# One transformer pair on one core: attention, value tiles, HGRN output and output projection put in another order on TensorE

## The reference

```python
# attention: 8 heads of 64, three dilated windows, merged by their softmax weights
for window, dilation in ((128, 1), (512, 4), (2048, 16)):
    o, l = dilated_window_attention(qh, kh, vh, window, dilation)   # softmax over keys t, t-d, ..., t-window
...
y = jnp.sum(softmax(lses)[..., None] * outs, axis=0)
# HGRN: 4 heads of 128; o = causal product of decayed scores with the values i
o = o * lax.rsqrt(jnp.mean(o * o, axis=-1, keepdims=True) + NORM_EPS)      # mean over the 128 of a head
o = o.reshape(B, S, HGRN_WIDTH) * norm_w
yb = o * jax.nn.silu(g)
...
mixed = jnp.concatenate([ya, yb], axis=-1)
h = h + jnp.einsum('bse,ed->bsd', mixed, w_out)
```

## Time and profile before

| | |
|---|---|
| median of three runs | 2258.12 us |
| the profiled execution | 2256.9 us, span 2255.1 us |
| TensorE busy | 2164.3 us, 96% |
| VectorE, ScalarE busy | 1521.4 us, 1073.4 us |
| granted TensorE clock, mean | 0.972 |
| last projection tile to end of output projection | 1657.2 to 1879.2 us of the span |

### The profile page before, as it was taken

How to read it: one execution, slowest core, us unless ns; L and a number is a source line. 1 busy time by engine, 2 the same in 40 slices (tenths; PEclk the granted TensorE clock), 3 DMA queues, 4 the chain that set the end, 5 groups by cost and what they waited for, 6 DMA issues and landing times.

```text
span 2255.1 us, 25922 instructions
## 1 busy us (share of the span) xinstructions
PE 2164.3 (96%) x8736; PEld 1432.9 (64%) x8736; DVE 1521.4 (67%) x1575; ACT 1073.4 (48%) x950; POOL 234.9 (10%) x239
## 2 busy tenths in 40 slices
PE   8999999999999999999999999689997899999998
PEld 3445457777777777777777777445643346888886
DVE  3953369999999999999999999544614633333333
ACT  1010147777777777777777777420002423222222
POOL 0003311112111111121211211100000000000000
PEclk9998989999999999999999999889998899999999
DMA  6123379999999999999999999611221011222220
GB/s 255 56 84 114 121 317 340 377 376 382 376 374 381 373 384 373 382 379 373 384 372 381 382 370 380 254 38 38 94 93 47 1 38 56 94 94 98 108 94 37
DMA packets 77756, 522.63 MB, mean 232 GB/s; under 512 B 10208, under 2 KB 10736, under 8 KB 21264
## 3 DMA queue, kind: packets, MB, share of 16 engines
q1 hardware_dynamic: 65088, 483.95, 55.4%
q0 software_dynamic: 9168, 31.01, 5.4%
q10 hardware_dynamic: 3456, 7.06, 1.0%
HBM read 500.98 MB, written 18.99 MB: 231 GB/s over the span
## 4 chain that ended last, share of the span: by engine, by line
PE 90%; DVE 7%; ACT 1%; DMA 1%; issue 1%; SPq 0%; DVEq 0%; ACTq 0%; POOLq 0%
PE bank L1006 21%; PE bank L1008 21%; PE bank L1007 21%; PE bank L872 13%; PE bank L1118 6%; DVE room L1301 3%; PE bank L1022 1%; PE bank L1133 1%; PE bank L1216 1%; PE bank L978 1%; PE bank L1014 1%; PE bank L881 1%; PE bank L1198 1%; DVE room L1640 1%; DVE room L1662 0%
## 5 line engine op out<-in xcount | busy, mean ns | idle before, releaser
L1448 DVE TENSOR_TENSOR ring_r<-ring,room_r 128x2048 fp32r<-128x2048 f32 x384 | 873.3, 2288 | 90.1 <-ACT room_r L626 87.3
L626 ACT ACTIVATE room_r<-ring 128x2048 fp32r<-128x2048 f32 x384 | 735.7, 1917 | 189.0 <-PE bank L1008 183.3
L1006 PE MATMUL bank<-room_r 128*96 128x512 f32 x1536 | 607.1, 395 | 3.5 <-DVE room_r L1480 1.9
L1008 PE MATMUL bank<-room_r 128*96 128x512 f32 x1536 | 603.1, 393 | 0.0
L1007 PE MATMUL bank<-ring_r,room_r 128*96 128x512 f32 x1536 | 603.0, 393 | 0.0
L1008 PEld LDWEIGHTS bank<-room_r 128*96 128x96 f32 x1536 | 248.8, 162 | 105.7
L1006 PEld LDWEIGHTS bank<-room_r 128*96 128x96 f32 x1536 | 248.9, 162 | 105.4 <-DVE ring_r L1448 4.4
L1007 PEld LDWEIGHTS bank<-ring_r,room_r 128*96 128x96 f32 x1536 | 249.0, 162 | 101.0 <-issue 0.2
L872 PE MATMUL bank<-ring,room 128*128 128x512 f32 x544 | 238.9, 601 | 4.0 <-ACT room L587 3.3
L872 PEld LDWEIGHTS bank<-ring,room 128*128 128x128 f32 x544 | 104.7, 194 | 134.5 <-issue 133.5
L1118 PE MATMUL bank<-room,ring 128*128 128x512 f32 x320 | 140.4, 597 | 0.0
(11 more groups left out here) (243 smaller groups left out, 2053.8 us busy)
## 6 DMA issues: line engine op xcount, KB each, us to landing
ring<-in_wmoe SPq DMA_DIRECT2D x384, 1024.0 KB, 11.6
ring<-in_wf SPq DMA_DIRECT2D x33, 1024.0 KB, 4.8
ring<-in_wp SPq DMA_DIRECT2D x9, 2048.0 KB, 7.8
ring<-in_wd SPq DMA_DIRECT2D x7, 2048.0 KB, 8.9
ring<-in_wd SPq DMA_DIRECT2D x3, 1024.0 KB, 8.1
room<-in_xT SPq DMA_DIRECT2D x2, 1024.0 KB, 8.4
room<-in_xtok ACTq DMA_DIRECT2D x1, 2048.0 KB, 7.7
h_rows<-room POOLq DMA_DIRECT2D x4, 512.0 KB, 3.1
```

What stands on the lines that cost most here:

```text
L626: act.activation(w_hi[s_ % PAIRS], raw_w[ORDER[s_]], ACT.Copy)\
L1006: pe.matmul(out, x_hi, w_hi, start=start, stop=False, skip_group_check=True)
L1008: return pe.matmul(out, x_lo, w_hi, start=False, stop=stop, skip_group_check=True)
L1448: dve.tensor_tensor(w_lo[i], raw_w[i], w_hi[s_ % PAIRS].bitcast(F32), ALU.subtract)\
```

## The change

**TensorE.** After the last projection tile it waits for all rotated tiles (`rot_done`, 8) and issues the scores of units 0 to 3 with 8 of the 64 value matmuls behind each. In each of the first 16 units two more value matmuls come first. HGRN output is made per token tile j, with `AT` as weights and tokens on partitions, ahead of units 17, 20, 23 and 26 (`O_AT`). `head_values` of a head moves from the end of its own units to the start of the next head's. After the last unit the output projection starts with three attention columns of groups 0 to 4; between them stand the last `head_values` and four transposes per token tile of the normed HGRN output (`hgrn_turn`); then the rest of all groups, each in a bank of its own.

**VectorE.** The mask `madd` now holds log(count)/SCALE where a key is allowed, so the product with `ctab` goes; `masked` takes a minimum of the negated scores, so that the separate scaling of the maximum goes; the sum comes from ScalarE's exponential. `masked` runs four units ahead, behind `weighted`; before, it ran two ahead, in front of it. The HGRN norm is one reciprocal of 128 x 16 and two products of 128 x 1024 at the end of the attention, and four products with the transposed output; `hg_norm` moves into the gate's product.

**ScalarE.** The exponentials run four units ahead and accumulate their sum. `probs_out` copies 512, 512 and 256 columns in place of 512, 384, 256 and 128. The value copies lie among the units, and after units 17, 20, 23 and 26 come a copy of 512 columns and four squares of 128 with their sums (`hgrn_evac`). One root of 128 x 16 stands behind the last `probs_out`.

**SP.** The table c2 is 1536 columns wide in place of 2048. The third feed-forward weight waits for the end of the scores and of `hgrn_turn`. The last norm's row is loaded during the feed-forward part, since its buffer holds attention output now.

```diff
+O_AT = [17, 20, 23, 26]
...
                 elif f == 2:
-                    sp.wait_ge(s["pn_ready"], HEADS * TT)
+                    sp.wait_ge(s["sc_done"], HEADS * TT)
+                    sp.wait_ge(s["oT_ready"], TT)
...
+            def hgrn_evac(j):
+                act.wait_ge(s["o_ready"], j + 1)
+                act.activation(on[:, j, :], bank[6][:, :], ACT.Copy)
+                for h in range(HG_HEADS):
+                    n = j * HG_HEADS + h
+                    ins = act.activation(junk[:, h * P:(h + 1) * P], bank[6][:, h * P:(h + 1) * P], ACT.Square, accum_out=hms[:, n:n + 1])
+                ins.then_inc(s["o_evac"], 1)
+
+            for u in range(AHEAD):
+                exps(u)
+                vt_out(u)
             for u in range(HEADS * TT):
                 h, i = divmod(u, TT)
+                if u + AHEAD < HEADS * TT:
+                    exps(u + AHEAD)
+                if i == 1 and h >= 1:
                     head_out(h - 1)
+                if i == 0 and 1 <= h <= TT:
+                    vt_out(TT + h - 1)
+                if u - 1 in O_AT:
+                    hgrn_evac(O_AT.index(u - 1))
+                if i == TT - 1:
+                    probs_out(h)
+            act.activation(hms, hms, ACT.Sqrt, bias=eps_rms, scale=1.0 / P).then_inc(s["ostd_ready"], 1)
             head_out(HEADS - 1)
...
+            pe.wait_ge(s["rot_done"], 8)
+            pe.wait_ge(s["p_evac"], 8)
             for u in range(AHEAD):
                 scores(u)
+                for k in range(KT):
+                    vt_step(u * KT + k)
             for u in range(HEADS * TT):
+                h, i = divmod(u, TT)
+                if u < 2 * KT:
+                    vt_step(TT * KT + 2 * u)
+                    vt_step(TT * KT + 2 * u + 1)
+                if u in O_AT:
+                    hgrn_out(O_AT.index(u))
+                if i == 0 and h >= 1:
+                    head_values(h - 1)
                 probs_T(u)
                 if u + AHEAD < HEADS * TT:
                     scores(u + AHEAD)
-                if u % TT == TT - 1:
-                    head_values(u // TT)
+            for g in range(2):
+                w_out(g, 0, 3)
+            head_values(HEADS - 1)
+            for g in range(2, 5):
+                w_out(g, 0, 3)
+            for j in range(TT):
+                hgrn_turn(j)
...
             def masked(u):
-                step(dve.tensor_tensor_reduce(sc[:, a4, 0:w], bank[u % 2][:, 0:w], madd[:, S - w:S], 1.0, NEG * 4,
-                                              ALU.add, ALU.max, top))
-                dve.tensor_scalar(bias, top, -SCALE, None, ALU.mult).then_inc(s["sc_done"], 1)
+                dve.tensor_tensor_reduce(sc[i], bank[u % 2][:, 0:w], madd[:, S - w:S], -SCALE, -NEG * 4,
+                                         ALU.add, ALU.min, att_s[:, i:i + 1]).then_inc(s["sc_done"], 1)
...
             def weighted(u):
-                step(dve.tensor_tensor_reduce(ex[:, a4, 0:w], ex[:, a4, 0:w], ctab[:, S - w:S], 1.0, 0.0,
-                                              ALU.mult, ALU.add, total))
                 step(dve.reciprocal(total, total))
-                dve.tensor_scalar(ex[:, a4, 0:w], ex[:, a4, 0:w], total, None, ALU.mult).then_inc(s["pn_ready"], 1)
-
-            for u in range(AHEAD - 2):
+                dve.tensor_scalar(ex[i], ex[i], total, None, ALU.mult).then_inc(s["pn_ready"], 1)
+
+            for u in range(AHEAD):
                 masked(u)
             for u in range(HEADS * TT):
-                if u + AHEAD - 2 < HEADS * TT:
-                    masked(u + AHEAD - 2)
                 weighted(u)
+                if u + AHEAD < HEADS * TT:
+                    masked(u + AHEAD)
```

More of the change, by code:

```diff
@@ L262, in build @@
         c2 = slot(3)
-        ctab, madd, cosT, sinT = (c2[:, n * S:(n + 1) * S] for n in range(4))
+        madd, cosT, sinT = (c2[:, n * S:(n + 1) * S] for n in range(1, 4))
         lmask = c2[:, 4 * S:4 * S + 8 * P].bitcast(I32).rearrange("p (l s) -> p l s", l=8)
@@ L754, in _, with vt_out @@
                            .then_inc(swap_in[m % 2], 16)
-            for g in range(8):
+            def vt_out(g):
                 act.wait_ge(s["vt_ready"], g + 1)
[L758 to L761, removed]
                 if g == 0:
                     act.wait_ge(s["lv_ready"], LEVELS + 1)
[L765 to L776, removed]
+                act.activation(v_tok[:, g, :] if g < 4 else i_tok[:, g - 4, :], bank[6 + g % 2][:, :], ACT.Copy)\
+                   .then_inc(s["vt_evac"], 1)
             def probs_out(h):
@@ L1153, in _, with vt_step @@
             p_tile(19)
-            for g in range(8):
+            def vt_step(n):
+                g, k = divmod(n, KT)
                 w = chunk2(pe, 5 + g // 4).rearrange("p (k c) -> p k c", k=KT)
-                if g < 2:
-                    pe.wait_ge(s["p_evac"], 7 + g)
-                else:
+                if k == 0 and g >= 2:
                     pe.wait_ge(s["vt_evac"], g - 1)
                 i = g % 4
-                accumulate(bank[g % 2][:, :], [(uT[:, k, i * P:(i + 1) * P], w[:, k, :]) for k in range(KT)])\
-                    .then_inc(s["vt_ready"], 1)
@@ L1165, in _ @@
[L1165 to L1173, removed]
-                ins.then_inc(s["o_ready"], 1)
@@ L1176, in hgrn_ms @@
[L1176 to L1190, removed]
+                ins = pe.matmul(bank[6 + g % 2][:, :], uT[:, k, i * P:(i + 1) * P], w[:, k, :], start=(k == 0), stop=(k == KT - 1))
@@ new lines, in vt_step, with hgrn_out @@
+                if k == KT - 1:
+                    ins.then_inc(s["vt_ready"], 1)
+            def hgrn_out(j):
+                pe.wait_ge(s["vt_evac"], 8)
+                pe.wait_ge(s["lv_copied"], LEVELS + 1)
+                if j >= 1:
+                    pe.wait_ge(s["o_evac"], j)
+                for h in range(HG_HEADS):
+                    for q in range(j + 1):
+                        ins = pe.matmul(bank[6][:, h * P:(h + 1) * P], AT[:, h, q, j * P:(j + 1) * P],
+                                        i_tok[:, q, h * P:(h + 1) * P], start=(q == 0), stop=(q == j), skip_group_check=True)
+                ins.then_inc(s["o_ready"], 1)
@@ L1192, in scores, with hgrn_turn @@
+            def hgrn_turn(j):
+                pe.wait_ge(s["on_ready"], j // 2 + 1)
+                if j >= 2:
+                    pe.wait_ge(s["hmix_ready"], j - 1)
+                for h in range(HG_HEADS):
+                    ins = pe.transpose(bank[6 + j % 2][:, h * P:(h + 1) * P], on[:, j, h * P:(h + 1) * P], ident)
+                ins.then_inc(s["oT_ready"], 1)
             def scores(u):
@@ new lines, in _ @@
+            for q in range(2):
+                part = on[:, 2 * q:2 * q + 2, :].rearrange("p j (h c) -> p (j h) c", h=HG_HEADS)
+                dve.tensor_tensor(part, part, hms[:, 8 * q:8 * q + 8].unsqueeze(2).broadcast_to([P, 8, P]), ALU.mult)\
+                   .then_inc(s["on_ready"], 1)
+            for j in range(TT):
+                dve.wait_ge(s["oT_ready"], j + 1)
+                dve.tensor_tensor(mix_hg[:, :, j * P:(j + 1) * P], bank[6 + j % 2][:, :].rearrange("p (h t) -> p h t", h=HG_HEADS),
+                                  hG[:, :, j * P:(j + 1) * P], ALU.mult).then_inc(s["hmix_ready"], 1)
@@ L1726, in _ @@
             for i in range(TT):
-                dve.wait_ge(s["ss4_ready"], 2 * i + 2)
+                dve.wait_ge(s["ss_ready"], 4 * TT + 2 * i + 2)
                 step(dve.reciprocal(rstd[:, 4 + i:5 + i], rstd[:, 4 + i:5 + i]))
```

123 lines of the change are left out of this document (64 added, 59 removed).

## The result

The changed kernel takes 2265.64 us (median of 6 runs, 2264.45 to 2266.81) against 2258.02 us before: ratio 1.0036, interval 1.0023 to 1.0049. It is 7.6 us slower. The forecast was 2268 us, slower. The profiled execution has a span of 2262.9 us, 7.8 more than before.

The account below looks back on a forecast made before the run. TensorE, busy 96% of the span, was taken as the bound, losing time in the norm and the attention's waits and clock. From 2256.9 us, -3.7 at full clock and +15.0 for clock gave 2268, range 2257 to 2275.

Parts of the forecast that it names:

- The new wait ahead: Behind the last projection, TensorE's first score waits for all eight rotated tiles and TensorE stands still: 10.8 us.
- Restart: After TensorE's idle time behind the projections, starting again from idle costs 1.4 us.
- Changes of shape: On TensorE, 0.15 us more wherever 64-row scores meet 128-row transposes; 80 such changes, 12.0 us.
- Borders of units 0 to 15: At three head borders `head_values` waits for ScalarE's `probs_out`, partly covered by value matmuls: three times 1.3, 3.9 us.
- Borders of units 16 to 31: Head borders without value matmuls, TensorE waiting for `probs_out`: 3.2 twice, 1.3 and 5.7 us, in all 13.3.
- TensorE and VectorE in turn: Units 16 to 27: transposes wait for divisions queued behind later masks; with HGRN matmuls waiting for ScalarE, 12.5 us.
- Clock: Units 16 to 31, 57% busy: lower level for 60% of the time, adding 15.0 us of a possible 25.
- Sum: Whole kernel: 3.7 us gained at full clock, 15.0 lost to the lower clock, +11.3 us in total.
- rival of a clock that holds: Units 16 to 31 keep the clock up: 2253.2 us, or 2249.8 if the swap lands early; chance 26%.
- lower level throughout: Units 16 to 31 run wholly at the lower clock, adding 25 us: 2278.2 us; chance 18%.
- VectorE's chain: Units 16 to 31: a rival said this chain does not bind, 25.8 us of waits gone, about 2227; chance 4%.
- The second rival: Units 16 to 31: the lower clock lasts longer than busy shares say, throughout at the extreme, 2278.2 us; chance 18%.

Follow-up runs that it names:

- the kernel with the mask alone: Kernel before with only the mask's new table, the minimum of negated scores and the sum from the exponential: 2245.54 us, ratio 0.9949.
- Three changes of order: Changed kernel with value matmuls ahead of the rotation wait, division ahead of the mask, copy ahead of the exponential: together 2229.9 us, ratio 0.9876.

## Why the prediction was right, step by step

- **The new wait ahead**: 10.8 forecast, 10.5 measured, ended by the rotation as said; taking it away with its restart was worth 12.6.
- **Restart**: 1.4 forecast, 2.3 measured.
- **Changes of shape**: 12.0 forecast in all, of which the clock's paragraph puts 5 in units 16 to 31. So 7 are left for units 0 to 15, the prologue and the output projection. A unit of two value matmuls, two transposes and a score of 256 columns took 2.76 us (1702.58 to 1705.34), 0.40 more than its passes (1.72, 0.21 and 0.43). Sixteen units at 0.40 and the prologue make about 8 without the output projection: the side of its estimate that the forecast priced at 2 more.
- **Borders of units 0 to 15**: 3.9 forecast, 0.97 + 0.97 + 1.11 measured.
- **Borders of units 16 to 31**: 13.3 forecast, 2.88 + 2.88 + 4.54 = 10.3 measured, with none ahead of unit 20, where 1.3 was forecast. There `hgrn_out(1)`, itself at the lower clock (3.67 us), ended at 1781.1, and ScalarE's copy had ended at 1780.3.
- **TensorE and VectorE in turn**: the mechanism as forecast, 12.5 us forecast and 7.9 measured (6.3 for the division, 1.4 and 0.15 for `hgrn_out`). The prediction doesn't split its 12.5. At its own prices (1.05, 1.26, 1.46) the six waits for the division that came are 7.5, which leaves 5.0 for `hgrn_out`. Each wait for the division is 0.2 shorter than its price, since the profile starts a wait behind the drain of the matmul ahead. The term that was mis-sized is `hgrn_out`'s, 5.0 against 1.55. In part this is `hgrn_evac`, which I had priced at 2.5 us (a copy and four squares with their sums at 0.5 each). The squares start 0.25 apart, and the whole takes 1.5:

```profile
1818.88 0.60 ACT L793 ACTIVATE ring<-bank 128x512 f32<-128x512 f32 x1
1819.37 0.27 ACT L796 ACTIVATE ring<-bank 128x128 f32<-128x128 f32 x1
1819.53 0.20 ACT L796 ACTIVATION_READ_ACCUMULATOR ring<-bank 128x1 f32 x1
1819.62 0.28 ACT L796 ACTIVATE ring<-bank 128x128 f32<-128x128 f32 x1
```

  So the border ahead of unit 28 was 4.54 and not 5.7. `hgrn_out(2)` waited 0.15 and `hgrn_out(3)` not at all; there the waits for the division helped too, for without them `hgrn_out` waited 2.7 us for the same squares (the run with the division ahead of the mask).
- **Clock**: 60% of the time at the lower level forecast, 64% measured (0.68), and 15.0 us forecast. From units 16 to 31, 69.4 us (1757.5 to 1826.9), take the forecast's 28.0 of work and 5 of shape changes, the 18.2 of measured waits, and 2 to 3 for the drains ahead of eleven waits: some 15 to 16 are left, and the estimate from the window gives 15.9. Both are arithmetic. What a run shows is that filling the waits gives back 7.1 us net of 17 added matmuls.
- **Luck in the clock's term**: the straight line joined two busy shares as the profile counts them, where matmuls slowed by the lower clock count for their longer time, but was read at 57%, a share at full clock. By the profile's count the stretch was 73% busy (49.80 of 68). Read there, the line gives 43% of the time, a clock of 0.78 and 10.8 us. Nor does one line hold: two stretches 82% busy were granted 0.83 (before, 1751 to 1824) and 0.76 (copy ahead of the exponential). That waits lower the clock was right and was shown; that the size came out was in part luck.
- **Sum**: +11.3 forecast, +7.8 between the profiled executions, +7.6 between the medians. The waits of units 16 to 31 were taken 7.6 us too long, some 5 when their drains are counted; restart and shape changes, taken too short, made up for 2 to 3 of it.

The rival of a clock that holds is out at 0.68, that of the lower level throughout at 64% of the time. VectorE's chain does bind. The second rival leaned on the rule of the Trainium skill (TensorE: Matmul & The Clock Gate, Part 4: PE-mode transpose) that transposes don't count as busy for the clock as other matmuls do. No run here decides on it: scores and transposes ran at 0.50 for 12 us in the kernel with the mask alone as well, while later heads, in which `head_values` stands between them, ran at 0.93. Which of the kinds of matmul the clock follows was not tried.

## What to carry to other kernels

When matmuls that wait for nothing are laid between dependent ones, look first at what they covered where they stood: here 55 us of value matmuls hid a rotation that ended 10.7 us behind the last projection. Where three in-order engines pass a unit on, an instruction for a later unit must not stand ahead of one that the next engine wants now: with a look-ahead of four units TensorE still waited 6.3 us where mask and division stood in the wrong order, and 12.2 us more than needed where exponential and copy did. And a wait on TensorE can cost more than its length, since the granted clock can fall with it, so a term for the clock belongs in the sum. It need not: three waits of 1 us among value matmuls left the clock at 1.00 (1700 to 1757), and taking away the 6.3 us for the division left it at 0.68.

## What the runs showed of the hardware that was not expected

Adding 17 matmuls to the waits made the kernel 7.1 us faster, with the granted clock at 0.89 in place of 0.68. The busy share alone does not tell the clock: 82% busy went with 0.83 in one kernel and with 0.76 in another. Three changes of order were worth 35.6 us singly and 35.7 together, 34.3 and 35.9 by the profiles' stretch. Of the three only the copy's moved the clock of units 16 to 31 by itself (0.76; 0.69 and 0.68 with the other two), and the three together gave 0.79.
